# The first twenty microseconds of a two-block transformer kernel: loads in halves and by row tiles, the root's table ahead, products of zeros, one table of small weights

## The reference, cut to what matters

```python
def rmsnorm(x, g):
    xf = x.astype(jnp.float32)
    y = xf * lax.rsqrt(jnp.mean(xf * xf, axis=-1, keepdims=True) + RMS_EPS)
    return (y * g.astype(jnp.float32)).astype(x.dtype)

def first_block(x, norm_g, w_in, ...):
    for l in range(DEPTH):
        h = rmsnorm(x, norm_g[l])
        c = split_columns(h @ w_in[l])
        ...
        y_a = flat(dilated_window_attention(heads(c["a_q"]), heads(c["a_k"]), heads(c["a_v"]), slopes_a))
        ...
            gate = jax.nn.sigmoid(h @ w_merge[l, i] + b_merge[l, i])
            merged = merged + gate * (y @ w_branch[l, i])
        x = x + merged @ w_out[l]
```

## Time and profile before

| | us |
|---|---|
| median of three runs | 2153.72 (2151.71 to 2154.66) |
| the profiled execution, span from first to last instruction | 2153.0 |
| TensorE busy | 1758.8 (82%) |
| VectorE busy | 595.3 (28%) |
| ScalarE busy | 390.8 (18%) |
| mean rate of the transfers | 250 GB/s |
| TensorE's first instruction | 11.68 |
| first scores of branch a | 49.87 |

### The profile page before, as it was taken

How to read it: one execution, slowest core, us unless ns; L and a number is a source line. 1 busy time by engine, 2 the same in 40 slices (tenths; PEclk the granted TensorE clock), 3 DMA queues, 4 the chain that set the end, 5 groups by cost and what they waited for, 6 DMA issues and landing times.

```text
span 2153.0 us, 30543 instructions
## 1 busy us (share of the span) xinstructions
PE 1758.8 (82%) x13354; PEld 1097.5 (51%) x13354; DVE 595.3 (28%) x1026; ACT 390.8 (18%) x753; POOL 36.0 (2%) x28
## 2 busy tenths in 40 slices
PE   6999999999999998765666598799987867766664
PEld 4788885779887664421222233676984422212221
DVE  1133312123421145411111112574345311211102
ACT  2324201313411134100000010251321100000001
POOL 0000000000000000000000000001030000000000
PEclk9999999999999999898888799899998988899877
DMA  9332333332334432999999999212014999999994
GB/s 340 98 96 98 137 137 144 139 87 98 118 118 176 176 118 83 413 427 427 427 427 427 426 371 417 104 74 90 4 49 188 400 428 426 427 427 428 428 426 186
DMA packets 51421, 538.72 MB, mean 250 GB/s; under 512 B 7440, under 2 KB 16272, under 8 KB 18224
## 3 DMA queue, kind: packets, MB, share of 16 engines
q1 hardware_dynamic: 49248, 527.06, 60.0%
q0 software_dynamic: 1152, 6.29, 0.8%
q10 hardware_dynamic: 848, 3.00, 0.4%
HBM read 535.28 MB, written 1.05 MB: 249 GB/s over the span
## 4 chain that ended last, share of the span: by engine, by line
PE 62%; DMA 29%; DVE 4%; ACT 3%; issue 2%; DVEq 0%; ACTq 0%
PE ps L415 52%; DMA arena<-in_moe_w_gu 17%; DMA arena<-in_moe_w_down 12%; PE ps L422 7%; PE ps L428 2%; DVE x L1423 1%; ACT arena L2240 1%; ACT hb L2236 1%; DVE arena L1412 1%; ACT L2236 0%; DMA vec<-in_vecs 0%; ACT hT L2236 0%; ACT arena L2236 0%; DVE hT L1435 0%; DVE arena L1427 0%
## 5 line engine op out<-in xcount | busy, mean ns | idle before, releaser
L415 PE MATMUL ps<-hT,ring 128*128 128x256 f32 (+2 forms) x1888 | 391.3, 372 | 0.0
L415 PEld LDWEIGHTS ps<-hT,ring 128*128 128x128 f32 (+2 forms) x1888 | 330.0, 184 | 53.6 <-issue 3.4
L422 PE MATMUL ps<-arena 128*32 128x512 f32 (+1 forms) x1572 | 242.2, 706 | 112.9 <-DMA arena<-in_moe_w_gu 89.7
L422 PE MATMUL ps<-ring,arena 128*32 128x512 f32 x1408 | 193.2, 679 | 95.2 <-DMA ring<-in_moe_w_gu 76.9
L2240 ACT ACTIVATE arena<-ps 128x512 f32<-128x512 f32 (+3 forms) x143 | 93.6, 654 | 851.6 <-PE ps L422 507.7
L415 PE MATMUL ps<-arena 64*64 64x64 f32 (+10 forms) x1944 | 183.3, 319 | 56.1 <-ACT arena L2511 22.3
L422 PEld LDWEIGHTS ps<-arena 128*32 128x32 f32 (+1 forms) x1572 | 55.9, 126 | 275.1 <-DMA arena<-in_moe_w_gu 131.6
L1412 DVE TENSOR_TENSOR arena<-arena,ps 128x256 f32<-128x256 f32 (+2 forms) x82 | 46.0, 561 | 541.1 <-ACT arena L2236 453.5
L415 PEld LDWEIGHTS ps<-arena 64*64 64x64 f32 (+4 forms) x1944 | 112.9, 158 | 127.6 <-ACT arena L2511 51.2
L422 PEld LDWEIGHTS ps<-ring,arena 128*32 128x32 f32 x1408 | 42.2, 116 | 227.2 <-DMA ring<-in_moe_w_gu 110.3
L415 PE MATMUL ps<-ring,hT 128*128 128x256 f32 (+4 forms) x576 | 149.5, 418 | 8.7 <-ACT hT L2236 7.0
(11 more groups left out here) (176 smaller groups left out, 1229.1 us busy)
## 6 DMA issues: line engine op xcount, KB each, us to landing
ring<-in_moe_w_gu SPq DMA_DIRECT2D x64, 2048.0 KB, 36.9
arena<-in_moe_w_gu SPq DMA_DIRECT2D x64, 2048.0 KB, 36.6
arena<-in_moe_w_down SPq DMA_DIRECT2D x32, 2048.0 KB, 36.2
ring<-in_moe_w_down SPq DMA_DIRECT2D x32, 2048.0 KB, 36.5
ring<-in_w_merge SPq DMA_DIRECT2D x16, 2048.0 KB, 7.4
ring<-in_w_in SPq DMA_DIRECT2D x10, 2048.0 KB, 7.4
ring<-in_attn_w_qkv SPq DMA_DIRECT2D x6, 2048.0 KB, 7.3
ring<-in_rw_w_rkv SPq DMA_DIRECT2D x6, 2048.0 KB, 7.4
```

Source lines behind the costliest of these rows:

```text
L415: i = t.matmul(o, l, r, start=first, stop=last, skip_group_check=True)
L422: i = t.matmul(o, l, r, start=first, stop=last, skip_group_check=True)
```

## The change

1. `x` is loaded by row tiles, each with a semaphore of its own: tile 0 first on ACT's queue, ahead of `tcom`; `vec` and tile 1 on SyncE's queue. Each engine waits only for the tile that it works on, and for `tcom` and `vec` only where it first uses them.
2. SyncE waits for nothing at the start. The first block of weights of layer 0 comes in two halves of four steps each, with two semaphores, and the eight steps of product 0 are split in two runs of four.
3. ACT computes the root of one zero before it waits for x, so that the table of functions with the root is loaded then. The squares that follow are in the same table.
4. GpSimd first fills 512 columns of `mT` with zeros, and TensorE multiplies them nine times, 256 columns each, into an accumulator tile that nothing reads.
5. The queries' and keys' small weights, `nsa_w2` and the positions are appended to the table `tfirst` on the host and come with it in one load (128 x 7104); the router weights `wr` are laid out on the host as they lie on the chip and come in one load. SyncE issues 5 loads where it issued 16 behind `in0`.

The core of the diff:

```diff
-    m.x_landed, m.consts_landed, m.first_landed = sem("x_landed"), sem("consts_landed"), sem("first_landed")
+    m.x_landed, m.consts_landed, m.first_landed = [sem(f"x_landed{i}") for i in range(NT)], sem("consts_landed"), sem("first_landed")
+    m.half_landed = sem("half_landed")
...
@@ TensorE, first_layer
-        t.wait_ge(*m.w.landed(L + "in1"))
         h_ready(0)
-        mm(lst[:KT], L + "a v0")
+        if l == 0:
+            t.wait_ge(m.half_landed, 16)
+            mm(lst[:4])
+        t.wait_ge(*m.w.landed(L + "in1"))
+        mm(lst[4 if l == 0 else 0:KT], L + "a v0")
...
@@ TensorE, start
+    t.wait_ge(*pool("zeros"))
+    mm([(ps.tiles[3][:, 0:256], m.mT[:, 0, 0:P], m.mT[:, 1, :], True, True) for _ in range(9)], "warm")
     t.wait_ge(m.consts_landed, 32)
-    t.wait_ge(m.x_landed, 16)
...
@@ ACT and DVE, norm_in
+        else:
+            s.wait_ge(m.x_landed[i], 16)
         fn(m.hb[:, i, :], x[:, i, :], ACT.Square, n + " sq", acc=ss)
...
+        s.wait_ge(m.consts_landed, 32)
         s.wait_ge(*pe(n))
...
@@ ACT, start
-    s.dma_start(x, T["x"].rearrange("b (t p) d -> p (b t) d", p=P)).then_inc(m.x_landed, 16)
+    s.dma_start(x[:, 0], T["x"][0, 0:P]).then_inc(m.x_landed[0], 16)
     s.dma_start(m.tcom, T["tcom"]).then_inc(m.consts_landed, 16)
-    s.dma_start(m.vec, T["vecs"]).then_inc(m.consts_landed, 16)
-    s.wait_ge(m.consts_landed, 32)
-    s.wait_ge(m.x_landed, 16)
+    s.wait_ge(*m.pool("zeros"))
+    fn(sml("tiny", 1)[0:1], m.mT[0:1, 0, 0:1], ACT.Sqrt)
...
@@ GpSimd, start
+    g.memset(m.mT[:, 0:2, :], 0.0).then_inc(*pool.one("zeros"))
     g.wait_ge(m.consts_landed, 32)
-    g.wait_ge(m.x_landed, 16)
...
@@ SyncE, first_tables and start
-        for dst, src in ((m.row, T["rows"]), (m.tfirst, T["tfirst"]), (m.tab["cz0"], T["cz0"]), (m.tab["cz1"], T["cz1"])):
+        for dst, src in ((m.row, T["rows"]), (m.tfirst, T["tfirst"]), (m.tab["cz0"], T["cz0"]), (m.tab["cz1"], T["cz1"]),
+                         (m.rw36, T["wr"])):
             y.dma_start(dst, src).then_inc(m.first_landed, 16)
             n += 16
-        for l in range(2):
-            y.dma_start(m.rw36[:, l], T["wr"][l].rearrange("(k p) n -> p k n", p=P)).then_inc(m.first_landed, 16)
...
-    y.wait_ge(m.consts_landed, 32)
-    y.wait_ge(m.x_landed, 16)
+    y.dma_start(m.vec, T["vecs"]).then_inc(m.consts_landed, 16)
+    y.dma_start(m.x[:, 1], T["x"][0, P:S]).then_inc(m.x_landed[1], 16)
...
-        cols(L + "in1", win, 512, 512, L + "a v")
+        if l == 0:
+            k = slot(L + "in1", L + "a v")
+            count[k] += 1
+            y.dma_start(ring[k][:, 0:2048], win[:, 4096:6144]).then_inc(m.half_landed, 16)
+            y.dma_start(ring[k][:, 2048:4096], win[:, 6144:8192]).then_inc(m.w.sems[k], 16)
+            landing(k, L + "in1")
+        else:
+            cols(L + "in1", win, 512, 512, L + "a v")
```

More of the change, by code:

```diff
@@ L276, in memory @@
     m.row = sb("row", T["rows"].shape[1])
-    m.rw36 = sb("rw36", 2 * KT * 36).rearrange("p (l k n) -> p l k n", l=2, k=KT)
+    m.rw36 = sb("rw36", 2 * KT * 36)
     m.lnr = sb("lnr", 2 * D).rearrange("p (a d) -> p a d", a=2)
@@ L300, in memory @@
         tab[k] = carve(tabs[k].shape[1])
-    m.tfirst = arena[:, 0:at[0]]
     m.w_uq = [carve(2 * 384).rearrange("p (k n) -> p k n", k=2) for _ in range(L1)]
@@ L305, in memory @@
     m.posT = [carve(32) for _ in range(L1)]
+    m.tfirst = arena[:, 0:at[0]]
     m.Sb, m.Pb, m.PTb = ([carve(512), carve(1024)] for _ in range(3))
@@ L545, in first_layer @@
         lst = proj_tok(hT, wcols(m.w(L + "in1"), KT, 512), KT, [o[:, i, :] for i in range(NT)], slice(0, 512))
+        h_ready(0)
+        if l == 0:
+            t.wait_ge(m.half_landed, 16)
+            mm(lst[:4])
         t.wait_ge(*m.w.landed(L + "in1"))
-        h_ready(0)
-        mm(lst[:KT], L + "a v0")
+        mm(lst[4 if l == 0 else 0:KT], L + "a v0")
         norm_in(l, 1)
@@ L764, in join @@
             t.wait_ge(*dve(name + " out b"))
-            mm([(p[:, 0:36], hT[:, k, i * P:(i + 1) * P], m.rw36[:, l, k, :], k == 0, k == KT - 1) for k in range(KT)], f"moe{l} route{i}")
+            mm([(p[:, 0:36], hT[:, k, i * P:(i + 1) * P], m.rw36[:, 36 * (KT * l + k):36 * (KT * l + k + 1)], k == 0, k == KT - 1) for k in range(KT)], f"moe{l} route{i}")
     def diff_attention():
@@ L1446, in norm_in @@
             tt(x[:, i, :], x[:, i, :], ps(f"l0 out{i}"), ADD, f"l0 x{i}")
+        else:
+            v.wait_ge(m.x_landed[i], 16)
         v.wait_ge(*act(n + " sq"))
@@ L1452, in norm_in @@
         p = ps(n)
+        v.wait_ge(m.consts_landed, 32)
         v.wait_ge(*pe(n))
@@ L2207, in rwkv @@
         join("rw", 1, 3, range(NT))
-    v.wait_ge(m.consts_landed, 32)
-    v.wait_ge(m.x_landed, 16)
     for l in range(L1):
@@ L3015, in layout @@
         "tcom": np.concatenate([tabs[k] for k in common], axis=1),
-        "tfirst": np.concatenate([tabs[k] for k in FIRST_TABLES], axis=1),
         "cz0": tabs["cz0"], "cz1": tabs["cz1"],
-        "pos": i["nsa_pos"].transpose(0, 1, 3, 2).reshape(L1, P, 32),
-        "wr": np.concatenate([i["moe_rg_w_2"], i["moe_re_w_2"]], axis=2),
+        "wr": np.concatenate([i["moe_rg_w_2"], i["moe_re_w_2"]], axis=2).reshape(2, KT, P, 36).transpose(2, 0, 1, 3).reshape(P, -1),
         "lora1": packed(np.concatenate([i["rw_w1_2"][0], i["rw_a1_2"][0], i["rw_g1_2"][0]], axis=1), (288,)),
@@ L3022, in layout @@
     }
-    for n in ("mla_w_uq", "mla_w_ukv", "nsa_w1", "nsa_w2", "rw_g2_2"):
+    uq, ukv = i["mla_w_uq"], i["mla_w_ukv"]
+    for n in ("nsa_w1", "rw_g2_2"):
         arrays[n] = i[n]
@@ L3032, in layout @@
         arrays[n] = a.transpose(0, 1, 4, 3, 2, 5).reshape(2, E // 2, P, -1)
+    uq = np.concatenate([uq, np.zeros((L1, 2 * P - 192, 384), np.float32)], axis=1).reshape(L1, 2, P, 384)
+    arrays["tfirst"] = np.concatenate([tabs[k] for k in FIRST_TABLES] + [uq[l].transpose(1, 0, 2).reshape(P, -1) for l in range(L1)] + [*ukv]
+                                      + [i["nsa_w2"][l].transpose(1, 0, 2).reshape(P, -1) for l in range(L1)]
+                                      + [i["nsa_pos"][l].transpose(0, 2, 1).reshape(P, 32) for l in range(L1)], axis=1)
     return {k: np.ascontiguousarray(a) for k, a in arrays.items()}
```

7 lines of the change are left out of this document (removed).

## The result

| | median us | lowest to highest | runs |
|---|---|---|---|
| before | 2154.75 | 2150.07 to 2160.01 | 19 |
| after | 2158.19 | 2153.06 to 2163.42 | 19 |

The ratio is 1.0015, 95% interval 1.0008 to 1.0022: slower by 3.2 us (1.7 to 4.7). That is less than the 4.3 us which the prediction took as the least that can be told from no change, but with 19 runs each the interval leaves zero out. Forecast was 6.8 us faster. In every run whose span was listed, of either kernel, the time stands 1.7 to 2.0 us above the span; the profiled execution of after has 2159.2.

A forecast was written before the change was run, and what follows sets the result against it. The prediction took TensorE to bound all that follows the start. Earlier transposes (3.5), a shorter way through hT (0.9) and a warm product 0 (2.4) sum to 6.8 us off, giving 2147.0 us, range 2144.3 to 2150.6.

The forecast's parts named there:

- The zeros ... 7.8 us if all are cold: TensorE's start: nine zero products end between 7 and 9 us; warmer clock and shorter hT wait together give 3.3 us.
- 6. Lookups ... change no instruction: zero: Part 6 of the sum: lookups of `rw36` and the packed layouts change no instruction, so zero gain or cost.
- Nothing on a transfer that comes at its own time: What follows the start: all hangs on TensorE, no transfer sets its own time, so an earlier start carries through.
- tcom at 8.1, bounds 6.9 and 9.7: Start: tcom lands at 8.1 us, so the transposes start at 8.2 instead of 11.68, worth 3.5 us.
- the case with 0.17: Start, rival: the clock falls before product 0 or zeros do not lift it; 2150.2 to 2149.3 us, chance 0.17.
- Weights at once: Product 0: first weight half lands at 10.3 and second at 12.8, in time for a start at 10.9; costs nothing.
- tile 1's chain: Norm of row tile 1: lies behind product 0 as before, its x there at about 8 us.
- small weights in one table: Loads ahead of the scores: landed at about 29 us, needed at 43; zero, with 14 us of cover.
- That the gain passes through the stage bound by transfers: Expert stage, 855 to 1350 us, DMA 0.99 busy: its weight stream waits for TensorE, so it starts earlier too.
- given back later: After the start, rival: gain lost in a wait for weights or in cold stretches falling elsewhere; 2153.7 us, chance 0.05.
- Whole transfers in turns: Start, rival: queues alternate by whole transfers, tcom at 6.9, first weight half ends last; 7.4 us gain, 2146.3, chance 0.15.
- the slower one: Start, rival: SP's queue served ahead of ACT's, tcom at 17.6, transposes at 17.7; 2159.7 us, chance 0.04.

The follow-up runs named there:

- e11: Changed kernel with the two rw_w_o loads issued only after the product rw v1: +1.9 us against the kernel before (-0.9 to +4.5).
- e5: Changed kernel plus 55 tiny products behind the first expert stage's router, making 128 added records with the zeros: -3.9 us against the kernel before (-6.0 to -1.9).
- e13: The changed kernel unaltered, run for a third profile: first product 7.13 us, `a qk` begins at 28.71; no total given.
- e3: Changed kernel with five products of zeros of 512 columns instead of nine of 256: -2.6 us against the kernel before (-4.5 to -0.6).
- e12: The changed kernel unaltered, run for a second profile: first product 10.12 us, `a qk` begins at 31.47; no total given.
- e6: Changed kernel with TensorE's early gaps filled by 64 products of zeros, large and tiny, 128 records: -1.7 us against the kernel before (-4.1 to +0.6).
- e7: As e6, with the identity's 256 columns of tcom loaded ahead of the rest: -2.8 us against the kernel before (-5.4 to -0.2).
- e9: Changed kernel with six 512-column zero products at start, two before product 0, 56 tiny pads behind the router: -3.7 us against the kernel before (-5.6 to -1.7).
- e10: As e9 with five zero products at start, 57 pads and the identity loaded first: 2148.39 against 2153.91 us, -5.8 (-8.2 to -3.4).
- e1: Changed kernel without its nine products of zeros: -2.4 us against the kernel before (-4.3 to -0.2).
- e4: Changed kernel with 64 products of zeros of 32 columns (128 records) instead of nine of 256: +17.9 us against the kernel before (+14.9 to +20.9).

## Why the prediction was wrong, point by point

1. "The zeros ... 7.8 us if all are cold", and "6. Lookups ... change no instruction: zero". This is the step that failed. I priced the zeros by their time and their clock and not as code: 36 more instructions at the head of TensorE's program cost 5.8 us 1460 us later. The first profile had shown such waits: "issue" is the third of TensorE's releasers, with 34.1 us in 15 waits, and I passed over it. Of these, twelve waits with 9.1 us lie on the ladder of 128 records, all in the RWKV stage. The other three, 25.0 us at records 5476, 5980 and 11860 in the expert stages, are something else, and it stays open what: in the change they are at the same records, 18 later only if the zeros are counted, so they moved with the program and not with the borders.
2. "Nothing on a transfer that comes at its own time" was false for the same reason. The transfers of code are such, and they stand in the page's table of queues (q8, 1.90 MB).
3. tcom at 8.1, bounds 6.9 and 9.7: it released the transposes at 9.57, 8.98 and 9.21 in the change's three profiles, 8.67 in e11 and 8.56 in e5. Inside the bounds, 0.5 to 1.5 us late. hb was ready at 7.4 (forecast 7.2), so the identity's landing was the limit, as said. This and the clock are the terms of the sum that were mis-sized. By the means of three profiles each, the transposes began 2.5 us earlier instead of 3.5, the way from there to the first product was 0.9 shorter, as forecast, and the products themselves 0.9 instead of 2.4: 4.2 us instead of 6.8. From 6.8 us faster to 3.4 slower, then, 2.6 us are the start, 5.8 the border, and 1.9 the rest, which is not settled.
4. The clock: the case with 0.17 (the clock falls again) happened in two of the change's three profiles, with the first product at 8.83 and 10.12 instead of 7.13 us. In e5 and e11, whose start is the same, it held. The wait for tcom ahead of the transposes was 0.33, 0.70 and 0.88 us where it held (e5, e13, e11) and 1.50, 1.85 and 2.12 where it fell (e3, after, e12), so the late tcom seems to have cost twice; no run changed this wait alone. With the gaps filled it held four times in four (e6, e7, e9, e10). Zeros without filling gave nothing where the clock fell: e1, which has none, began `a qk` the same 3.6 us earlier than the kernel before.
5. Weights at once, tile 1's chain, small weights in one table: right. Between the transposes and the first scores TensorE waited for no load (the gap ahead of the scores still ends on ACT, 1.52 us).
6. That the gain passes through the stage bound by transfers: right as far as the intervals go, by e4 (17.7 in, 17.9 out, 14.9 to 20.9) and e10 (6.8 less 2 for pads in, 5.8 out, 3.4 to 8.2).
7. The rivals: the forecast's mechanism reached the start with 4.2 us on average. The one called "given back later" had the right form, but the 5.8 us came by neither of its two mechanisms. Whole transfers in turns, with tcom at 6.9, did not occur, nor did the slower one (SP's queue ahead of ACT's, tcom at 17.6): tcom landed at 9.53, 8.94 and 9.16 in the change's three profiles, behind x's second half on SP's queue (7.57, 7.93 and 7.81), as with turns of single packets.

The Trainium skill has the rule that I should have weighed, in "Runtime: NRT & Kernel Launch", section "Instruction fetch mechanics": code is fetched in blocks of 16 KiB, 256 instructions, by a queue of the sequencer's own, and crossing a border is "mostly hidden". The trace agrees on the block (128 records with their weight loads between waits, packets of 16 KB) and on "mostly", but the rest costs 9.1 us in twelve waits in the RWKV stage of the kernel before, and 14.6 us in thirteen in that of the change; and the fetch that met a load of weights was late by 2.5 us more.

## What to carry to other kernels

Where a long unrolled program has bursts of short instructions (here 15 ns a record), count the instructions that an edit adds ahead of them, on that engine, and see where the block borders fall. The list of "issue" waits by record number, before and after, shows it: with the added records counted, waits for code keep their places (7345, 7473), while waits of another kind move with the program. Padding to a whole block (256 instructions) in a place where the engine idles took the shift back here. In this kernel the start could be judged only with the borders held fixed. And the products of zeros held the clock in four profiles of four where no gap was left between them and the real work, and in three of six of the changed kernel where gaps were left (e4 left aside, whose zeros had not lifted the clock).

## What the runs showed of the hardware

- TensorE's code arrives in packets of 16 KB per 256 instructions: 116 packets, and 117 with 128 records more. At 15 ns a record a block lasts about 2 us; a lone fetch showed 1.31 us of waiting, one beside a 2 MB load of weights 3.8 us, in all four profiles that had the border there with that load in flight (3.82, 3.80, 3.77, 3.82).
- A wait of 3.8 us without work brought the clock down for what followed (granted 0.92 and 0.79, 15.70 instead of 14.00 us for 32 records), one of 1.31 us did not (1.00 and 14.00).
- Products of 128 x 128 weights with 32 columns took 0.21 us a record in e4, half of one with 512 columns at 2.4 GHz (0.43), for a sixteenth of the columns. The weight loads were busy all of that time (10.00 of 10 us), and the clock was at the lower level by the transposes behind them (1.95 us, like the cold ones of the earlier trace rows). Products of 32 x 32 weights took 0.055 us a record in e5, at a granted clock of 0.50.
- Two queues of the hardware shared the engines as GpSimd's had the earlier trace rows, near enough: from 0 to 9 us the change moved 1.33 MB on ACT's, which is all that it held, and 1.49 MB on SP's.
